# Reordering the start, one DMA group and the turn to attention in a fused decoder-step kernel

## The reference

```
h = rmsnorm(x, norm_mix);  z = h @ w_in              # columns: qa ka va fa | bu bv | qc kc vc | qm
qa, ka, qc, kc, qm = rmsnorm per head of 64 channels (gains qk_gain)
logf = log_sigmoid(fa + b_f)
A: causal softmax attention, 4 heads, bias = cumulative sum of logf      (prompt and paged samples)
B: u * (W_s v + b), gelu halves, W_s lower triangular per chunk of 128
C: dilated window attention, 4 heads, three branches with relative bias
M: attention into 256 memory tokens; mk, mv = rmsnorm(mem) @ w_mem_kv
x += rmsnorm per group(concat(A, B, C, M)) @ w_out;  x += ConvFFN(rmsnorm(x))
```

## Time and profile before

| | us |
|---|---|
| runs | 1368.9, 1367.58, 1368.24; median 1368.24 |
| profiled execution, its own time | 1366.95 |
| its span, first to last instruction | 1365.2 |
| PE busy | 1306.8 (96%) |
| DVE busy | 947.3 (69%) |
| ACT busy | 553.3 (41%) |
| POOL busy | 218.9 (16%) |
| mean granted clock of PE | 0.985 |

### The profile page before, as it was taken

One profiled execution on the slowest core, in us unless ns is written; L12 is line 12 of the kernel. 1 busy time (PEld: TensorE's weight loads), 2 busy tenths in 40 slices (PEclk: granted clock), 3 DMA queues, 4 the chain that ended last, 5 costly groups with the idle time before them and its releaser, 6 DMA issues.

```text
span 1365.2 us, 24259 instructions
## 1 busy us (share of the span) xinstructions
PE 1306.8 (96%) x9271; PEld 1201.5 (88%) x9271; DVE 947.3 (69%) x1388; ACT 553.3 (41%) x906; POOL 218.9 (16%) x221
## 2 busy tenths in 40 slices
PE   7998999979979999999899999999999999999999
PEld 5787887857767677999899999999999999999999
DVE  6568889979988867567777878877978895111111
ACT  6623121155557666343553444354454354100100
POOL 0420025333322540100111111011011000000000
PEclk9999999989999999999899999999999999999999
DMA  9768765789999773421222222222222284322222
GB/s 304 262 211 224 210 188 176 208 234 270 288 317 318 248 218 100 150 93 63 70 86 93 70 71 94 71 70 93 72 69 93 77 306 142 114 74 90 74 74 74
DMA packets 151067, 206.82 MB, mean 151 GB/s; under 512 B 12860, under 2 KB 112724, under 8 KB 150672
## 3 DMA queue, kind: packets, MB, share of 16 engines
q1 hardware_dynamic: 133108, 146.48, 34.9%
q0 software_dynamic: 12848, 46.73, 10.9%
q10 hardware_dynamic: 4996, 12.07, 3.2%
HBM read 174.91 MB, written 29.82 MB: 150 GB/s over the span
## 4 chain that ended last, share of the span: by engine, by line
PE 61%; DVE 15%; DMA 8%; issue 5%; POOL 3%; SPq 3%; ACT 2%; ACTq 2%; DVEq 0%; POOLq 0%
PE ps L1322 8%; PE ps L1323 8%; PE ps L1324 8%; PE ps L1383 6%; PE ps L1384 6%; PE ps L1385 6%; PE ps L1163 3%; DMA upr<-in_w_upL 2%; PE ps L1066 2%; PE ps L1067 2%; PE ps L1068 2%; PE ps L1186 2%; POOL rsn L2729 1%; DMA ring<-in_cache_c_k 1%; PE ps L1145 1%
## 5 line engine op out<-in xcount | busy, mean ns | idle before, releaser
L1322 PE MATMUL ps<-hhi,uph 128*128 128x258 f32 x704 | 202.0, 287 | 5.7 <-issue 3.8
L1323 PE MATMUL ps<-hlo,uph 128*128 128x258 f32 x704 | 200.3, 284 | 0.0
L1324 PE MATMUL ps<-hhi,upl 128*128 128x258 f32 x704 | 200.1, 284 | 0.0
L2630 DVE TENSOR_TENSOR dnl<-dnr,dnh 128x896 fp32r<-128x896 f32 (+2 forms) x24 | 27.3, 1136 | 173.8 <-ACT dnh L1819 173.8
L1322 PEld LDWEIGHTS ps<-hhi,uph 128*128 128x128 f32 x704 | 134.8, 192 | 7.4 <-issue 4.0
L1323 PEld LDWEIGHTS ps<-hlo,uph 128*128 128x128 f32 x704 | 135.1, 192 | 0.0
L1066 PE MATMUL ps<-whi,hhi 128*128 128x512 f32 (+1 forms) x336 | 127.4, 379 | 7.6 <-DVE fa L1993 2.6
L1324 PEld LDWEIGHTS ps<-hhi,upl 128*128 128x128 f32 x704 | 134.5, 191 | 0.0
L1068 PE MATMUL ps<-whi,hlo 128*128 128x512 f32 (+1 forms) x336 | 125.5, 374 | 0.0
L1067 PE MATMUL ps<-wlo,hhi 128*128 128x512 f32 (+1 forms) x336 | 125.1, 372 | 0.0
L1383 PE MATMUL ps<-fh,dnh 128*128 128x344 f32 x336 | 107.5, 320 | 1.8 <-DVE dnl L2630 1.8
(11 more groups left out here) (341 smaller groups left out, 3586.7 us busy)
## 6 DMA issues: line engine op xcount, KB each, us to landing
upr<-in_w_upL SPq DMA_DIRECT2D x88, 256.0 KB, 3.4
ring<-in_cache_a_k SPq DMA_DIRECT2D x168, 128.0 KB, 3.4
scr_act<-va SPq DMA_DIRECT2D x22, 516.0 KB, 2.6
ring<-in_cache_a_k ACTq DMA_DIRECT2D x88, 128.0 KB, 3.1
wst<-in_w_in SPq DMA_DIRECT2D x32, 256.0 KB, 4.2
fr<-scr_act SPq DMA_DIRECT2D x14, 516.0 KB, 5.1
dnr<-in_w_down SPq DMA_DIRECT2D x12, 448.0 KB, 4.1
dnr<-in_w_down SPq DMA_DIRECT2D x10, 512.0 KB, 3.9
```

Of the source, the lines that this page charges most:

```text
L1322: pe.matmul(out, hi_, r_hi[:, cs], start=(first and i == 0), stop=False, skip_group_check=not first)
L1323: pe.matmul(out, hi_, r_lo[:, cs], start=False, stop=False, skip_group_check=not first)
L1324: m = pe.matmul(out, lo_, r_hi[:, cs], start=False, stop=(i == 3), skip_group_check=not first)
```

## The change

1. **First units.** For (5,0), (5,1), (0,0), (0,1) and (0,2) DVE does `reduce_sq(k)` ahead of `finish_norm(pending)`.
2. **Bias transfers.** `bias_part(0..3)` moves from units (1,"S"), (1,0), (1,1), (1,2) of ACT to (3,1) to (3,4). In (1,6) SP loads all four pages of the granule, ACT none. `early_softmax` is taken apart: `new_key` beside the last unit, `forget_bias` after the first score, `maxima` at step 2.
3. **Head 0 inside the last unit.** Storage of the attention operands is laid out at 8256 bytes per pair of rows, so that the first 896 columns of head 0 lie over what (4,7) doesn't read. `first_hi` and `first_lo` make these while PE runs (4,7); the tail (tile 7) goes through `cut_tails` and is made after it. `qk(0)` stands inside (4,7), after kc = 5. Head 0 begins with tile 6, tile 7 is its third step. DVE, ACT and POOL do their part of (4,7) later; its ACT eviction copies all columns, so that PE's bank comes free before `finish_norm`.
4. **What goes with it.** Banks of blocks 2 to 4 are turned by two, weight slots by eight; the V load of pair 0 goes to (4,3) on SP; POOL issues the first four V gathers ahead of the root of (4,7); V sums begin at step 6 instead of 4 (14 of them in the memory heads instead of 12), with the maxima's exchange two steps later.

The diff, cut to its core (`...` where lines are left out; the function `side_by_side` and the loop over the units of PE are only moved below `qk`, with `wslot` and the lines shown):

```diff
+        row2 = [hoff + 8 * COLS * i for i in range(7)]
+        CUT = NT - 1
+        FREE = CUT * P
...
-        bank = {k: (6 if k[1] == "S" else prompt_no[k] % 4) for k in units}
+        bank = {k: (6 if k[1] == "S" else (prompt_no[k] + 2 * (k[0] in (2, 3, 4))) % 4) for k in units}
+        def wslot(q):
+            return (q + 8) % NW
-        BIAS_PART = {units[units.index((0, 7)) + 1 + q]: q for q in range(4)}
+        BIAS_PART = {(3, q + 1): q for q in range(4)}
+        ALTERNATE_0 = [6, 0, 7, 1, 5, 2, 4, 3]
-        VA, VM = 28, 40
+        V0 = 6
+        VA, VM = 4 * NT - V0, 40
-        TURN_MAX = {1: 0, 33: 1, 46: 2, 57: 3}
-        SEND_MAX = {2: 0, 34: 1, 47: 2, 59: 3}
+        TURN_MAX = {3: 0, 33: 1, 46: 2, 57: 3}
+        SEND_MAX = {4: 0, 34: 1, 47: 2, 59: 3}
... SP
-                    load_pages(sp, kpool, n // 8, n % 8, n % 4, (0, 1))
+                    load_pages(sp, kpool, n // 8, n % 8, n % 4, range(4) if k == (1, NT - 2) else (0, 1))
+                if k == (4, 3):
+                    sp.wait_ge(S("w_used"), 5 * KC)
+                    for s4 in range(4):
+                        uses = [m for m in prompt_no if prompt_no[m] % 4 == s4 and m[0] in (0, 1, 5)]
+                        sp.wait_ge(S(f"zo_out{s4}"), 16 * sum(n_out[m[0]] for m in uses))
+                    v_load(0)
             sp.wait_ge(S("z_done"), NU)
-            v_load(0)
             k_load(NKP + 2)
             c_rows(1)
             qk_load(1)
             outputs(units[NU - 2])
+            k_load(NKP + 3)
             outputs(units[NU - 1])
-            k_load(NKP + 3)
... PE
             def qk(g):
+                if g < 2:
+                    T_.wait("act_z", UI[units[NU - 3 + g]] + 1)
+                    T_.wait("dve_z", DI[units[NU - 3 + g]] + 1)
+                if g == 2:
+                    T_.wait("tail_lo", 1)
+                    T_.wait("c_tail", 16)
+                    T_.wait("q_ones", 2)
...
+            CUT_KC = 5
+                    if k == units[NU - 1] and kc == CUT_KC:
+                        qk(0)
...
-            pe.wait_ge(S("dve_z"), len(dve_units))
-            pe.wait_ge(S("act_z"), NU)
-            pe.wait_ge(S("q_ones"), 1)
... ACT
+                    if u == NU - 1:
+                        act.activation(dst[:, c0:c0 + nh * HD], z[:, c0:c0 + nh * HD], ACT.Copy, scale=rx)
                     m = act.activation(sq[0:r, NI[k] % 2, 0:nh * HD], z[:, c0:c0 + nh * HD], ACT.Square, scale=rx)
-                for n in K_ASK[u]:
+                for n in () if k == (1, NT - 2) else K_ASK[u]:
+            def tail_copy(i, piece):
+                T_.wait("p_lo", PN[(0, piece)])
+                act.activation(cut_tails[:, i, :], ps[0:HD, FIRST[piece], FREE - 512:512], ACT.Copy).then_inc(S("tail_cp"), 1)
+            def tail_hi():
+                T_.wait("tail_cp", 2)
+                act.activation(khh[HD:P, 0, FREE:SEQ], cut_tails[:, 0, :], ACT.Copy)
+                act.activation(khh[0:HD, 0, FREE:SEQ], cut_tails[:, 0, :], ACT.Copy)
+                act.activation(qhl[0:HD, 0, FREE:SEQ], cut_tails[:, 1, :], ACT.Copy, scale=gcol(0, 0))
+                act.activation(q1c[0:HD, 0, FREE:SEQ], cut_tails[:, 1, :], ACT.Copy, scale=gcol(0, 0)).then_inc(S("tail_hi"), 1)
             for piece in FIRST:
-                hi(0, piece)
+                first_hi(piece)
+            tail_copy(0, "k1")
+            tail_copy(1, "q1")
             act.activation(fb[:, 0:1], fb[:, 0:1], ACT.Exp)
+            ex(0)
+            act.wait_ge(S("z_done"), NU)
+            act.dma_start(klc[HD:HD + 2, 0, FREE:SEQ].bitcast(f32), scr_c[0][:, FREE:SEQ]).then_inc(S("c_tail"), 16)
+            tail_hi()
+            evict(NU - 1, units[NU - 1])
... DVE
+            FIRST_UNITS = [(5, 0), (5, 1), (0, 0), (0, 1), (0, 2)]
-            for u, k in enumerate(units):
+            for u, k in enumerate(units[0:NU - 2]):
+                if k in FIRST_UNITS:
+                    reduce_sq(k)
                 if pending:
                     finish_norm(pending)
-                if b in NORM:
+                if b in NORM and k not in FIRST_UNITS:
                     reduce_sq(k)
-                if k == (4, 5):
-                    early_softmax()
...
+            reduce_sq(units[NU - 2])
+            new_key(0)
+            first_lo("k0")
+            finish_norm(units[NU - 3])
+            first_lo("k1")
+            first_lo("q1")
+            finish_norm(units[NU - 2])
+            first_lo("q0")
...
+            score(0)
+            forget_bias(0)
+            tail_lo()
+            reduce_sq(units[NU - 1])
...
+                if g == 2:
+                    lo(1, "k0")
+                    dve.wait_ge(S("p_lo"), PN[(1, "k0")])
+                    dve.memset(ps[:, 7, 0:WG], 0.0).then_inc(S("dve_set"), 1)
+                    dve.wait_ge(S("dve_set"), 7)
+                    maxima(0, 0, 4)
+                if g == 4:
+                    finish_norm(units[NU - 1])
-                if g == 2:
+                if g == 4:
                     subtract_a(0)
... POOL
+                if k == units[NU - 2]:
+                    pool.wait_ge(S("rs_norm"), len(norm_units) - 2)
+                    pool.wait_ge(S("z_done"), NU - 1)
+                    pool.memset(q1c[HD:HD + 2, 0, 0:FREE].bitcast(f32), 1.0).then_inc(S("q_ones"), 1)
                 if k == units[NU - 1]:
                     pool.wait_ge(S("z_done"), NU)
-                    pool.memset(q1c[HD:HD + 2, 0, :].bitcast(f32), 1.0).then_inc(S("q_ones"), 1)
+                    pool.memset(q1c[HD:HD + 2, 0, FREE:SEQ].bitcast(f32), 1.0).then_inc(S("q_ones"), 1)
+                    pool.wait_ge(S("g_rows"), 1)
+                    for n in range(4):
+                        v_load(n)
```

More of the change, by code:

```diff
@@ L496, in qtile @@
             H, s = divmod(g, NT)
-            return s if not two(H) else ALTERNATE[s] if H + 1 < len(HEADS) else NT - 1 - s
+            return s if not two(H) else ALTERNATE_0[s] if H == 0 else ALTERNATE[s] if H + 1 < len(HEADS) else NT - 1 - s
         big_to = [0]
@@ L1009, in prep, with slot_free, qk @@
                 m.then_inc(S("p_tp"), 1)
+            def slot_free(g):
+                if g >= 2:
+                    T_.wait("s_nm" if two((g - 2) // NT) else "s_exp", g - 1)
+            def qk(g):
+                H, s = divmod(g, NT)
+                W = P * nblk(g)
+                if g < 2:
[5 more added lines that the diff above has]
+                    T_.wait("q_ones", 2)
+                if s == 1 and two(H):
+                    T_.wait("p_lo", PN[(H, "q0")])
+                if s == 4 and not two(H):
+                    T_.wait("p_lo", PN[(H, "q1")])
+                if s == 0:
+                    T_.wait("p_lo", PN[(H, "q1" if two(H) else "q0")])
+                    if HEADS[H][0] == ATT:
+                        T_.wait(f"c_ld{H % 2}", 16 * (H // 2 + 1))
+                        T_.wait("q_ones", 1 if H == 0 else 3)
+                    else:
+                        T_.wait("q_ones", H % 2 + 4)
+                slot_free(g)
+                if g in (48, 60):
+                    T_.wait("gmax", 3 if g == 48 else 4)
+                if g == 58:
+                    T_.wait("mx", 4)
+                p, bank_ = H % 2, 2 * (g % 2)
+                if two(H):
+                    q0 = qtile(g) * P
+                    for c in range(0, W, 512):
+                        w = min(512, W - c)
+                        out = ps[:, bank_ + c // 512, 0:w]
+                        pe.matmul(out, qhl[:, p, q0:q0 + P], khh[:, p, c:c + w], start=True, stop=False)
+                        i = pe.matmul(out, q1c[0:HD + 2, p, q0:q0 + P], klc[:, p, c:c + w], start=False, stop=True)
+                else:
+                    q_ = qhl if s < 4 else q1c
+                    for a in range(2):
+                        q0, c = a * 512 + (s % 4) * P, a * NMEM
+                        out = ps[:, bank_, c:c + NMEM]
+                        pe.matmul(out, q_[:, p, q0:q0 + P], khh[:, p, c:c + NMEM], start=True, stop=False)
+                        i = pe.matmul(out, q_[0:HD + 2, p, q0:q0 + P], klc[:, p, c:c + NMEM], start=False, stop=True)
+                i.then_inc(S("s_qk"), 1)
+            CUT_KC = 5
             def side_by_side(group):
@@ L1215, in _ @@
                 piece = prep_piece(H, s)
-                if piece:
+                if piece and g not in (0, 2):
                     prep(H + 1, piece)
-                if g < STEPS:
+                if 0 < g < STEPS:
                     qk(g)
+                if g in (0, 2):
+                    prep(1, piece)
                 mine = V_AT.get(g, ())
```

197 lines of the change are left out of this document (92 added, 105 removed).

## The result

The change takes the kernel from 1368.87 us (median of 20 runs, 1362.44 to 1376.16) to **1358.79 us** (median of 20, 1353.41 to 1364.73); the ratio is **0.9921, 95% interval 0.9904 to 0.9938**, that is 10.8 us less by the ratio, with 8.5 to 13.1 as its interval, and 10.1 less by the two medians. A later series of six runs of the same program gave 0.9896 (0.9873 to 0.992). 1358.2 had been forecast. The sum was right, but by the traces two of its terms were wrong and cancelled: part 3 doesn't cost the 3.0 us that it was charged with, and part 4 brings nothing up to step 6. Behind step 6 single executions differ too much to tell.

A forecast was written before the change was run, and what follows sets the result against it. PE, busy 96% of the span, was taken as the bound, so gains are PE gaps closed: -3.85 -7.4 +1.0 +3.0 -2.8 = -10.05 us against 1368.24 gave 1358.2 us, range 1353.0 to 1364.5.

The forecast's parts named there:

- part 3: Block 3: the moved bias transfers make DVE 1.5 us later, so PE waits at block 4's start; +3.0 us.
- part 4: Turn to the attention steps: head 0 inside the last unit removes DVE idle time; -2.8 us, bounds 1.0 and 4.8.
- Part 1: First units: `reduce_sq` ahead of `finish_norm` removes PE's gap before (0,4) and the half-rate stretch; -3.85 us.
- Part 2: Block 1 to block 2's second unit: bias transfers leave ACT's queue; -7.4 us, +1.0 for late DMA.
- Rival 3: DMA engines set the pace of block 1 and the first memory-head steps; 6 us gained, 1362.2; chance 0.20.
- rival 2: No price in block 3 or block 1, since DVE arrives with lead; 14 us gained, 1354.2; chance 0.20.
- PE already waits 0.33 us for DVE's split at 226.55: Start of block 4: DVE's split already late, so 1.5 us more lateness makes PE wait 1.8 us.
- The added wait holds nothing: Inside (4,7): `first_lo("q1")` is done about 276.5, PE arrives at 276.9, so PE loses nothing.
- So the gain is DVE idle time. Of the 7.5 us idle I keep 4.6: Attention start, 272.6 to 302.2: DVE's work is conserved, 4.6 us of idle stays, score(5) comes 2.9 us sooner.
- Part 5: Memory-head steps: V sums two steps later, two of them moving to steps 35 and 37; nothing for PE.
- Rival 5: Memory heads: 14 V gathers in 16 steps set the pace and cost 14 us; slower, 1372; chance 0.05.
- Rival 4: ACT's evictions wait for `zo` and the tail chain takes the 4.6 us; 1 to 2.5 us gained, 1366.5; chance 0.10.

The follow-up runs named there:

- e1_reduce: The kernel before with only the squares of the first five prompt units reduced ahead of the preceding product; ratio 0.9982 (0.9961 to 1.0003).
- e2_bias: The kernel before with only the bias transfers moved to units (3,1) to (3,4) and the page loads of (1,6) on SP; ratio 0.9976.
- e3_both: The kernel before with the early reduces and the moved bias transfers, without head 0 inside the last unit or later V sums; ratio 0.9939.
- e4_qk_end: The changed kernel with the matmuls of step 0's scores behind the last unit's last kc instead of its sixth; ratio 0.9922.
- e12_fill_ahead: The kernel of `e3_both` plus identity transposes on PE: 34 inside the 4.6 us wait, 16 behind the scores of step 1; ratio 0.989.

## Why the prediction was right, and where it was not

**Part 1** (-3.85): unit (1,"S") came 4.01 us sooner, in `e1_reduce` 3.6. The wait and the half-rate stretch both went, the reduce of (0,0) ended at 47.16 (49.1 forecast). Right.

**Part 2** (-7.4, +1.0 for the DMA engines, so -6.4): from (1,"S") to the second unit of block 2 32.03 us for 38.86, so -6.83; `e2_bias` has its last unit 6.4 us sooner. Right, with the +1.0 too high: no gap of PE or DVE in block 1 named a DMA, and the DMA share fell from 0.83 to 0.80 instead of rising. Rival 3, by which the DMA engines would set the pace of block 1, fell. The rule of the Trainium skill that had spoken for it ("DMA: Bandwidth & Descriptors", section "Issuing engines are not separate DMA queues": another issuer saves sequencer time only) is not contradicted: sixteen transfers at 0.62 us hold ACT's queue for 9.9 us, and the 6.8 gained lie below that.

**Part 3** (+3.0): refuted; PE lost 0.3 us between block 2 and block 4 (10.84 and 10.54 in the table). The step that failed is "PE already waits 0.33 us for DVE's split at 226.55". The lateness itself was sized right: DVE stands 9.04 us sooner than before at the splits (216.74 for 225.78) while PE is 10.54 sooner, so 1.5 us later against PE.

DVE, the kernel after:

```profile
216.74 2.49 DVE L1965 TENSOR_TENSOR wlo<-wst,whi 128x512 fp32r<-128x512 f32 x4
```

But these four are for kc 4 to 7. PE began kc 0 at 216.01 with slices split long ago in (3,0) to (3,3), and came to kc 4 at 218.86; the first of the four was done by 217.5. So the 0.33 us was not a wait for this split, though the profile puts it down to one: a wait of 0.30 stood in before also ahead of block 1 (83.27) and block 2 (112.74), and at block 4 it was 0.30 again after the change, now put down to a `zo`. It was there to be seen. At block 4 the lateness is hidden behind some 1.4 us of cover, and rival 2 (no price in block 3) described this part, with its 0.20.

The lateness doesn't vanish, though. DVE carries it through block 4 into the last unit. Its `forget_bias`, before and in `e3_both`:

```profile
272.51 0.68 DVE L2090 TENSOR_TENSOR sA<-sA,biasA 128x512 f32<-128x512 f32 x1
...
265.39 0.68 DVE L2090 TENSOR_TENSOR sA<-sA,biasA 128x512 f32<-128x512 f32 x1
```

In before it starts 0.23 us ahead of the last unit, in `e3_both` 1.28 us behind its start. DVE's work from U to step 6 is 24.8 us in before, 26.2 in `e2_bias` and 26.5 in `e3_both`. In those two it fits into idle time; part 4 had counted on the same idle time.

The other thing missed is small: the wait for the mixing product in block 2 grew from 1.03 to 1.42 us, behind a page load on SP that DVE waited 3.50 us for (2.81 in before), and another 1.5 to 2 us go when the clock falls behind it. The prediction had said that it is wrong if PE waits inside (4,7) or if DMA waits appear in blocks 1 to 3; the first came true, and of the second this one wait of DVE, longer than before.

**Part 4** (-2.8): 0 up to step 6, by traces; in the whole kernel not resolved. Two steps of the forecast failed. "The added wait holds nothing" was wrong: PE stood 1.74 us in the unit, since DVE had the sum of its last granule, two `reduce_sq`, `new_key` and a product ahead of it, and was done with `first_lo("q1")` 5.9 us into the unit (267.49 + 0.61) and not 3.8 ("done about 276.5", the unit starting at 272.74). This cost nothing in itself (`e4_qk_end`).

The step that mattered is "So the gain is DVE idle time. Of the 7.5 us idle I keep 4.6". Its list of waits was good in part (1.8 us for the tail copies, measured 1.81). But the idle time that it set out from had other owners. Some of it was PE's half rate: without part 4 and with the clock held, DVE idles only 4.2 us (`e12_fill_ahead`), where before has 7.9. Some of it, 1.4 to 1.7 us, DVE's lateness from parts 2 and 3 had already filled (26.2 and 26.5 us of work for 24.8). Part 4 itself adds 0 to 0.6 us of work to that (27.0, 26.4 and 26.4 us in after, its second execution and `e4_qk_end`), for in before `forget_bias`, `new_key` and `maxima` ran at 272.51 to 275.77, beside the last unit (272.74) and not "before the last unit". With both gone, part 4 has little idle time left to remove: 4.2 us without it, 3.7 with it.

The forecast had used a clock that stays up only as the far bound of this part (4.8), and had not asked what the half rate does to the kernel without part 4. The clock alone is not the cause either, since it costs both kernels 2 us or more and with it held both come within 0.25 us of each other. What bounds the 30 us that are left stays open.

**Part 5** (0): the time from step 6 to the end varied by 20 us between executions, and no difference can be put down to the later V sums. Rival 5 (slower by 14 us there) is excluded by the ratio of the whole. Rival 4 is, too: its 1366.5 is outside the interval.

So -4.0 -6.8 +0.3 and 0 make -10.5; -10.05 was forecast and 10.8 (8.5 to 13.1) measured. The agreement to 0.6 us is luck of two errors of 3 us against each other, as far as the traces up to step 6 show; with only one of them the time would have been 3 us off and still inside the range.

## What to carry to other kernels

Before a small wait is read as "this engine is at its edge", look whether the same wait stands at other block starts, and follow which slice the waiting instruction needs first: the releaser in the row is inferred, and here it was not the one that held. Work started sooner is worth something only where the work behind it is not held by something else; here 6 us at the first score became nothing six steps later. Before idle time is counted as a gain, ask who owns it: a slower clock beside it, or lateness that another part of the same change will put there. And when the engine that is 96% busy falls to half rate behind waits of 1 to 2 us, spare matmuls into free banks gave some 5 us more here (two intervals that just overlap) at a few lines of code. Behind the wait instead of inside it, 34 of them delayed the first score by 4 us.

## What the runs showed of the hardware

In block 2, one wait between 512-column matmuls, 0.89 to 1.70 us long in eleven traces, was followed by a half-rate stretch in three of them (behind 1.43, 1.67 and 1.70 us) and not in the others (1.48 and less). The first and the second trace of after, which are one program, differ in the same way near 400 us. So the price of one wait is its own length plus, some of the time, 1.5 to 2 us in the projection or more in the steps. The runs of one program differ by 11 us (after, 1353.4 to 1364.7 in twenty), and in these twenty the slower ones tend to have the lower mean clock (correlation -0.75). That fits the clock as a part of it, and doesn't prove it. The two stretches at half rate in the steps of after lasted 6.8 us each, though PE was busy without a pause from 0.3 us behind their start (from 278.94 and from 289.17); the first one of its second execution lasted some 10 us.
